# The first two weight chunks of a two-layer encoder trunk: one after the other, or together k by k

## What is computed

```
def rmsnorm(x, g):
    xf = x.astype(jnp.float32)
    xf = xf * lax.rsqrt(jnp.mean(xf * xf, axis=-1, keepdims=True) + EPS)
    return (xf * g.astype(jnp.float32)).astype(x.dtype)

def swiglu(h, w_gate, w_up, w_down):
    return (jax.nn.silu(h @ w_gate) * (h @ w_up)) @ w_down
```

## Time and profile before

| | us |
|---|---|
| median of three runs | 1929.72 |
| the profiled execution's own time | 1929.98 |
| its span | 1928.2 |
| PE busy | 1912.7 |
| DVE busy | 997.4 |
| ACT busy | 610.5 |
| DMA, share of 16 engines | 29.3% |

### The profile page before, as it was taken

The page is one execution under the profiler, slowest core; times in us unless marked ns, Lnnn a source line. Parts: engine busy times, 40 slices in busy tenths (PEclk is TensorE's granted clock), DMA queues, the critical chain, the costliest instruction groups (busy, mean ns, idle before and its releaser), DMA issues.

```text
span 1928.2 us, 31368 instructions
## 1 busy us (share of the span) xinstructions
PE 1912.7 (99%) x12436; PEld 1742.1 (90%) x12436; DVE 997.4 (52%) x1588; ACT 610.5 (32%) x822; POOL 53.1 (3%) x68
## 2 busy tenths in 40 slices
PE   9999999999999999999999999999999999999998
PEld 8999999999999999999999999999898888888887
DVE  7655543357656555543365555433556654444333
ACT  5323222224333223222232322222423332232321
POOL 0000000000000000000000000000023000000000
PEclk9999999999999999999999999999999999999999
DMA  7322223332122222233322223233322223233331
GB/s 200 105 89 96 86 83 91 95 123 66 66 89 88 87 95 90 84 90 90 95 88 91 94 87 92 83 90 95 97 66 66 78 97 98 89 96 94 91 90 53
DMA packets 55337, 175.70 MB, mean 91 GB/s; under 512 B 6692, under 2 KB 12100, under 8 KB 55272
## 3 DMA queue, kind: packets, MB, share of 16 engines
q1 hardware_dynamic: 54712, 174.36, 29.1%
q10 hardware_dynamic: 560, 0.42, 0.1%
HBM read 171.35 MB, written 3.41 MB: 91 GB/s over the span
## 4 chain that ended last, share of the span: by engine, by line
PE 98%; DVE 1%; DMA 0%; SPq 0%; ACT 0%; issue 0%; DVEq 0%; ACTq 0%
PE psum L1164 35%; PE psum L1174 19%; PE psum L1172 10%; PE psum L1177 10%; PE psum L1173 10%; PE psum L1176 10%; DMA rb_sb<-in_rel_bias 0%; PE psum L1316 0%; PE psum L1206 0%; PE psum L1451 0%; PE psum L1361 0%; PE psum L1365 0%; SPq L324 0%; PE psum L1461 0%; PE psum L1463 0%; PE psum L1462 0%
## 5 line engine op out<-in xcount | busy, mean ns | idle before, releaser
L409 ACT ACTIVATE wh<-raw 128x1024 fp32r<-128x1024 f32 x254 | 269.1, 1060 | 775.9 <-PE psum L1164 392.2
L752 DVE TENSOR_TENSOR wl<-raw,wh 128x1024 fp32r<-128x1024 f32 x326 | 400.8, 1230 | 217.9 <-ACT wh L472 143.1
L1164 PE MATMUL psum<-xs,wh 128*128 128x264 f32 (+1 forms) x1824 | 426.0, 337 | 0.0
L1174 PE MATMUL psum<-xs,wh 128*128 128x512 f32 x1056 | 415.0, 393 | 0.0
L1164 PEld LDWEIGHTS psum<-xs,wh 128*128 128x128 f32 x1824 | 293.4, 188 | 40.7 <-issue 3.8
L1172 PE MATMUL psum<-xs,wh 128*128 128x272 f32 x1056 | 305.6, 289 | 2.7 <-DVE xs L769 2.7
L1177 PE MATMUL psum<-xs,wl 128*128 128x272 f32 x1056 | 304.1, 288 | 0.0
L1173 PE MATMUL psum<-xs,wh 128*128 128x272 f32 x1056 | 303.6, 288 | 0.0
L1176 PE MATMUL psum<-xs,wl 128*128 128x256 f32 x1056 | 296.0, 280 | 0.0
L1164 PE MATMUL psum<-xs,wl 128*128 128x264 f32 (+1 forms) x912 | 264.5, 334 | 0.0
L1177 PEld LDWEIGHTS psum<-xs,wl 128*128 128x128 f32 x1056 | 198.3, 188 | 45.5
(11 more groups left out here) (244 smaller groups left out, 2149.6 us busy)
## 6 DMA issues: line engine op xcount, KB each, us to landing
raw<-in_w_gate_up SPq DMA_DIRECT2D x175, 512.0 KB, 3.5
raw<-in_w_down SPq DMA_DIRECT2D x64, 448.0 KB, 3.3
raw<-in_w_down SPq DMA_DIRECT2D x32, 512.0 KB, 3.5
raw<-in_od_in SPq DMA_DIRECT2D x21, 512.0 KB, 3.5
raw<-in_ev_in SPq DMA_DIRECT2D x18, 512.0 KB, 3.5
raw<-in_ev_out SPq DMA_DIRECT2D x8, 512.0 KB, 3.4
raw<-in_od_out SPq DMA_DIRECT2D x8, 512.0 KB, 3.5
x<-in_x_t SPq DMA_DIRECT2D x8, 264.0 KB, 5.3
```

Of the source, the lines that this page charges most:

```text
L409: act.activation(wh[:, slot, :], raw[:, slot, :], ACT.Copy).then_inc(wh_ready, 1)
L752: dve.tensor_tensor(wl[:, slot, :], raw[:, slot, :], f32(wh[:, slot, :]), ALU.subtract).then_inc(wl_ready, 1)
L1164: last = pe.matmul(dst, weights[:, slot, w], both[:, part, k, tok], start=start and p == 0, stop=stop and p == 2)
L1174: pe.matmul(psum[:, 2 * acc_at + 1, :].rearrange("p (h t) -> p h t", h=2), wh[:, slot, w], both[:, :, k, b], start=start, stop=False, skip ...
```

## The change

The first two chunks are multiplied together. For every k, as x arrives, PE does the block of chunk 0 and then that of chunk 1 (`first_pair`). Both chunks are fetched, copied and taken apart in halves: the halves for k 0 to 3 first, the second halves ahead of x piece 4. The table's product moves behind the pair. Twelve matmuls of ones are done first instead of ten.

```
                 if q == 0:
-                    sp.dma_start(raw[:, 0, 0:CW // 2], w_gu[0, :, 0:CW // 2]).then_inc(half_in, 16)
+                    sp.dma_start(raw[:, 0, 0:CW // 2], w_gu[0, :, 0:CW // 2]).then_inc(half_in[0], 16)
                     for m in range(KT):
-                        if m == 2:
-                            sp.dma_start(raw[:, 0, CW // 2:CW], w_gu[0, :, CW // 2:CW]).then_inc(raw_in[0], 16)
-                        if m == 6:
-                            load(1, w_gu[1])
+                        if m == 1:
+                            sp.dma_start(raw[:, 1, 0:CW // 2], w_gu[1, :, 0:CW // 2]).then_inc(half_in[1], 16)
+                        if m == 4:
+                            for c in range(2):
+                                sp.dma_start(raw[:, c, CW // 2:CW], w_gu[c, :, CW // 2:CW]).then_inc(raw_in[c], 16)
                         sp.dma_start(x[:, m, :], x_dram[:, m, :]).then_inc(x_in[m], 16)
...
             for m in range(KT):
-                if m == 2:
-                    act.wait_ge(raw_in[0], 16)
-                    act.activation(wh[:, 0, CW // 2:CW], raw[:, 0, CW // 2:CW], ACT.Copy).then_inc(wh_ready, 1)
-                if m == 6:
-                    high(1)
+                if m == 1:
+                    act.wait_ge(half_in[1], 16)
+                    act.activation(wh[:, 1, 0:CW // 2], raw[:, 1, 0:CW // 2], ACT.Copy).then_inc(half_high, 1)
+                if m == 4:
+                    for c in range(2):
+                        act.wait_ge(raw_in[c], 16)
+                        act.activation(wh[:, c, CW // 2:CW], raw[:, c, CW // 2:CW], ACT.Copy).then_inc(wh_ready, 1)
                 act.wait_ge(x_in[m], 16)
                 split_x(0, m)
...
             for m in range(KT):
-                if m == 2:
-                    dve.wait_ge(wh_ready, 1)
-                    dve.tensor_tensor(wl[:, 0, CW // 2:CW], raw[:, 0, CW // 2:CW], f32(wh[:, 0, CW // 2:CW]),
-                                      ALU.subtract).then_inc(wl_ready, 1)
+                if m == 1:
+                    dve.wait_ge(half_high, 2)
+                    dve.tensor_tensor(wl[:, 1, 0:CW // 2], raw[:, 1, 0:CW // 2], f32(wh[:, 1, 0:CW // 2]),
+                                      ALU.subtract).then_inc(half_low, 1)
+                if m == 4:
+                    for c in range(2):
+                        dve.wait_ge(wh_ready, c + 1)
+                        dve.tensor_tensor(wl[:, c, CW // 2:CW], raw[:, c, CW // 2:CW], f32(wh[:, c, CW // 2:CW]),
+                                          ALU.subtract).then_inc(wl_ready, 1)
                 low_x(0, m)
-            for n in range(1, RING):
+            for n in range(2, RING):
                 low(n)
...
-                for c in range(4):
+                if q == 0:
+                    first_pair()
+                for c in range(0 if q else 2, 4):
                     free(t + c)
                     if c == 3:
                         pe.wait_ge(var_ready, v + 1)
                     from_x(base + c, t + c, v, real=real, first=c == 0, between=first_sums if q == 0 and c == 2 else None, wide=not real)
-                    if c == 0 and q == 0:
-                        table_product()
...
+            def first_pair():
+                for k in range(KT):
+                    pe.wait_ge(xl_ready, k + 1)
+                    for c in range(2):
+                        if k == 0:
+                            pe.wait_ge(half_low, c + 1)
+                        if k == KT // 2:
+                            pe.wait_ge(wl_ready, c + 1)
+                        last = ffn_passes(c, c, k, xs, k, k == 0, k == KT - 1)
+                        if k == KT - 1:
+                            last.then_inc(chunk_done, 1)
+                table_product()
+
...
             pe.wait_ge(ones_set, 1)
-            for _ in range(10):
+            for _ in range(12):
                 pe.matmul(psum[:, 7, 0:P], ones[:, :], ones[:, :], start=True, stop=True)
```

More of the change, by code:

```diff
@@ L232, in trunk @@
         gains_in, table_in, const_in = sem("gains_in"), sem("table_in"), sem("const_in")
-        half_in, half_high, half_low = sem("half_in"), sem("half_high"), sem("half_low")
+        half_in, half_high, half_low = [sem("half_in0"), sem("half_in1")], sem("half_high"), sem("half_low")
         raw_in = [sem(f"raw_in{j}") for j in range(RING)]
@@ L501, in _ @@
             act.dma_start(g_sb[:, :], gains).then_inc(gains_in, 16)
-            act.wait_ge(half_in, 16)
+            act.wait_ge(half_in[0], 16)
             act.activation(wh[:, 0, 0:CW // 2], raw[:, 0, 0:CW // 2], ACT.Copy).then_inc(half_high, 1)
@@ L1179, in from_x @@
             def from_x(n, tile, v=None, more=0, real=False, first=False, between=None, wide=False):
[L1181 to L1185, removed]
+                pe.wait_ge(wl_ready, more + (n + 1))
                 outs = parts(acc_slot(tile), real)
                 for k in range(KT):
-                    if halved and k == KT // 2:
-                        pe.wait_ge(wl_ready, 1)
                     if first:
```

## The result

The changed kernel takes 1933.20 us (median of 20 runs, 1932.38 to 1934.86) against 1929.55 (20 runs, 1928.96 to 1930.80): a ratio of 1.002, with an interval from 1.0013 to 1.0027. It is 3.65 us slower. The profiled execution took 1933.16 us with a span of 1931.4, against 1929.98 and 1928.2.

A forecast was written before the change was run, and what follows sets the result against it. PE, busy 99% of the span, was taken to bound the kernel. 1929.98 (profiled) + 1.35 for later sums + 1.5 for the clock gave 1932.8, or 1932.6 against the median; range 1930.5 to 1934.5 (8 in 10).

The forecast's parts named there:

- The pair: Start on PE: chunk 1's first block at 7.75, PE never late after k = 1, both chunks done at 18.9.
- The ones: Start on PE: twelve matmuls of ones end at 6.2 instead of 5.3, at a cost of 0 to 0.1 us.
- The stall: Middle of chunk 2: PE stands still 4.25 us for the sum of squares, held behind the table's product on ACT.
- the term of 1.35: PE's sums in chunk 2 start at 26.75 instead of 25.39, 1.35 us later.
- The clock: PE's clock falls to 1.2 GHz at about 25.1, during the stall, and is low to 29.7.
- the term of 1.5: Behind the stall, 3.0 us past the restart run at half speed: 1.5 us lost, bounds 0 and 2.3.
- Rival (d): Only the stall's clock fall, low from the restart or longer: 2.3 to 3.2 us lost, 1933.4 to 1934.3; chance 20%.
- the count from the fall: Behind the stall: 4.64 us at the low clock counted from its fall, so low to 29.7, 1.5 us lost.
- The estimate by Part 1: Behind the stall: full clock returns after about 4 us of sustained matmuls, 2.0 us lost, a sum of +3.4.
- (a): The clock holds through the stall in chunk 2: 1931.1 us; chance 18%.
- (b): No stall in chunk 2, the gain of 2.85 us is kept: 1926.9 us; chance 3%.
- (c): Clock falls first in the sparse start, the pair loses 2.3 us, then again at the stall: 1935.3; chance 9%.

The follow-up runs named there:

- the version with three moves: Changed kernel with the table's product inside the pair ahead of k = 6, its copy behind ACT's second square, the sums one block later: 1927.56 us (0.9990).
- the kernel with the stall filled: Changed kernel with 18 matmuls of ones on PE ahead of the wait for the sum of squares: 1931.58 us (1.0012).
- the product late: Kernel before, without a pair, with the table's product behind chunk 1 instead of chunk 0: 1935.33 us (1.0031).

## Why the prediction was right, point by point

Forecast 1932.6, with 1930.5 to 1934.5; measured 1933.20.

- **The pair.** Right in kind: after the first blocks PE was never late. Its end was put at 18.9; 18.5 in the profile of the changed kernel, 19.0 to 19.6 in the five others that have the product at the pair's end. The step behind it is the landing of chunk 1's first half. I took 6.25 from the third transfer of the kernel before. With the new order ACT began its copy at 5.25 in the changed kernel's profile; in two of the ten profiles with this order before 5.6, in the other eight at 6.4 to 6.9; so one row stood for a time that varies by over 1 us.
- **The ones.** Their cost of 0 was right for the kernel before (1929.50 with twelve). In the changed kernel's profile they held the first block by 0.2 us: x's low part was ready at 5.97 and the block began at 6.20. It took 7.51 - 6.20 = 1.31 us, so the full clock came only during it. What I left out was their use. The fall of the clock in the sparse start is shown with ten ones in the version with three moves, where it is worth 0.3 us by the medians (1927.88 against 1927.56). How much of the 1.35 us between ten and twelve in the changed kernel is due to it stays open. I had argued that the kernel before, just as sparse, kept its clock; with ten ones the hole behind the first block was 1.2 us, against 0.64 before.
- **The stall.** Shown by two separate moves: 4.25 forecast, 4.0 measured; it shrinks to 1.1 when the product is moved and to 0.7 when its copy is. Sums put at 26.75, 26.31 in the profile. By the medians, though, the term of 1.35 is 2.1 (the kernel with the stall filled), because the half usually lands later than I took it.
- **The clock.** The fall was put at 25.1, at 24.4 it came; the term of 1.5 is 1.6 by the medians, 2.4 in the one profile, where the clock stayed low for 4.87 us of work. Rival (d)'s "counted from the restart" describes that execution; the count from the fall describes the median. So the clock's term of 1.5 came out right partly by luck. It rested on a fall 2.6 us after PE stops and on 4.64 us at the low level. In four profiles the fall came 2.1 (twice), 3.5 and 4.3 us after PE had stopped at the sums, and the clock stayed low for 6.8 us in two of them and 3.4 in the other two. The sums' term was the mis-sized one, 1.35 against 2.1, and it makes most of the 0.6 by which the forecast fell short.
- **The rule of the Trainium skill.** "TensorE: Matmul & The Clock Gate", section "Why this matters for your kernels", gives gaps over some 3 us as what sends the clock down. The stalls here agree: 2.2 us did not in the profile, 3.1 and 4.0 did. The estimate by Part 1 of that page of the Trainium skill, +3.4, was closer to the measured 3.65 than my +2.85, but it doesn't follow that its 2.0 for the clock was better: it stands on the same 1.35 for the sums, and by the medians the clock cost 1.6. And the start shows more than the rule: 1.21 us of idle time, with 0.49 shortly before, brought a fall too.
- **Rivals.** (a), the clock holds: 1931.1, refuted by the trace; its own kernel (the filled stall) gives 1931.6. (b), gain kept: 1926.9; the version that keeps it reaches 1927.6. (c), the early fall: seen with ten ones in the version with three moves. Four of the changed kernel's twenty runs, from 1934.0 to 1934.9, lie high; an early fall or a longer low stretch at the stall would fit them, and no trace shows which.
- **The line between no change and slower.** I had put it at 1933.6 and gave no change 0.78. The interval leaves no doubt that the change is slower, by 0.19%, a hair under the line.

## What to carry to other kernels

Before you move an instruction behind more work on its engine, list who waits for it in program order on the others, and what stands behind that wait: here a matmul of 0.6 us held eight squares, which hold the sums. When one engine gets ahead, ask where its next wait is and move that point along too; a gain of 3 us turned into a stall of 4. And count a stall of several us on PE as more than itself, since what runs after it may run at half speed: work without use in the hole was worth 1.6 us.

## What the runs showed of the hardware

- The clock fell with a stall of 3.1 us (one profile) and of 4.0 (three), not with one of 2.2 (one). It also fell without any long stall when PE had idle times of 0.49 and 1.21 us around a single block, while it held in another profile with 0.32 and 1.17. What it takes isn't a single idle time.
- In one profile the clock fell only after the stall was over, 0.3 us into the work behind it.
- What a fall costs varied with the execution. By half of the work done at the low level it was 2.4 us in the changed kernel, 2.9 with 4 matmuls in the stall, 1.5 in the changed kernel with ten ones, 1.7 with the product late and 1.7 in the sparse start.
- The third transfer of the queue, issued at 1.68 to 1.70 us, was followed by ACT's copy at 5.25 to 6.93 us in the ten profiles with the same order of issues. In the profiles of the changed kernel and of the one with the product in the pair, that put chunk 1's first block 0.4 us later (7.51 and 7.92).
